# Experts in pairs, one in each column half of the array, over a ring of twelve staging slots

## What is computed

```python
N_EXPERTS, N_GROUPS, TOP_K, D_FF_EXPERT = 16, 4, 2, 512

def grouped_moe(h, router_w, router_bias, w_gate, w_up, w_down):
    t = h.reshape(B * S, D)                        # 256 tokens x 1024
    scores = sigmoid(t @ router_w)
    ...                                            # best group of 4 experts, the top 2 experts in it
    gates = ...                                    # 256 x 16, two entries a row are not zero
    for e in range(N_EXPERTS):
        he = silu(t @ w_gate[e]) * (t @ w_up[e])   # 1024 -> 512
        out = out + gates[:, e:e + 1] * (he @ w_down[e])   # 512 -> 1024
```

## Time and profile before

| | |
|---|---|
| runs | 2398.96, 2403.47, 2403.6 us; median 2403.47 |
| the profiled execution | 2399.3 us, of which the span is 2397.5 |
| TensorE busy / granted clock, mean | 2188.3 us (91%) / 0.955 |
| VectorE, ScalarE busy | 1468.1 us (61%), 884.0 us (37%) |
| DMA | 592.65 MB, mean 247 GB/s |
| first expert layer, first up matmul to the residual | 1660.54 to 1926.54 |
| second expert layer, the same | 2124.65 to 2388.08 |

### The profile page before, as it was taken

One profiled execution on the slowest core, in us unless ns is written; L12 is line 12 of the kernel. 1 busy time (PEld: TensorE's weight loads), 2 busy tenths in 40 slices (PEclk: granted clock), 3 DMA queues, 4 the chain that ended last, 5 costly groups with the idle time before them and its releaser, 6 DMA issues.

```text
span 2397.5 us, 28486 instructions
## 1 busy us (share of the span) xinstructions
PE 2188.3 (91%) x10492; PEld 1627.1 (68%) x10492; DVE 1468.1 (61%) x2294; ACT 884.0 (37%) x1093; POOL 62.3 (3%) x93
## 2 busy tenths in 40 slices
PE   3999899988998998999979998877999989889998
PEld 3788787867886887888867887654555467655553
DVE  6888777647896887766658986764212167532112
ACT  3344545544344343545534334421211244211111
POOL 0000000000000000000000001100000011000000
PEclk9999999999999999999999999877999989889999
DMA  8997443436995896444327993411999954149997
GB/s 345 387 375 306 157 165 141 139 112 236 367 370 196 322 376 245 175 150 152 130 88 292 362 363 130 154 42 55 373 388 396 407 195 159 45 149 379 390 386 292
DMA packets 86337, 592.65 MB, mean 247 GB/s; under 512 B 9680, under 2 KB 13136, under 8 KB 15568
## 3 DMA queue, kind: packets, MB, share of 16 engines
q1 hardware_dynamic: 79760, 579.90, 62.3%
q10 hardware_dynamic: 6464, 11.19, 1.4%
HBM read 590.00 MB, written 1.05 MB: 247 GB/s over the span
## 4 chain that ended last, share of the span: by engine, by line
PE 80%; DVE 10%; ACT 4%; DMA 3%; issue 2%; POOL 1%; DVEq 0%; SPq 0%; POOLq 0%; ACTq 0%
PE gu L2096 12%; PE acc L1807 11%; PE acc L1810 10%; PE acc L1811 10%; PE tr L2096 10%; PE gu L1807 6%; PE gu L1811 6%; PE gu L1810 6%; PE acc L2096 5%; PE tr L1870 3%; DVE w_lo L1000 2%; DMA proj<-ada_stream 2%; DVE proj L1072 1%; ACT pair L564 1%; DVE tf L1666 1%
## 5 line engine op out<-in xcount | busy, mean ns | idle before, releaser
L1000 DVE TENSOR_TENSOR w_lo<-stage,w_hi 128x2048 fp32r<-128x2048 f32 x240 | 547.9, 2286 | 57.9 <-ACT w_hi L526 57.6
L526 ACT ACTIVATE w_hi<-stage 128x2048 fp32r<-128x2048 f32 x240 | 457.3, 1911 | 273.3 <-PE acc L1811 261.1
L1072 DVE SCALAR_TENSOR_TENSOR proj<-proj,c_row 128x1024 f32<-128x1024 f32 x240 | 291.6, 1218 | 49.2 <-DMA proj<-ada_stream 39.2
L1807 PE MATMUL acc<-w_hi,hT_hi 128*128 128x512 f32 (+1 forms) x736 | 308.5, 419 | 6.2 <-DVE hT_lo L1368 5.1
L1807 PE MATMUL gu<-w_hi,hT_hi 128*128 128x512 f32 x704 | 283.0, 402 | 10.0 <-DVE pair L1148 9.5
L1810 PE MATMUL acc<-w_lo,hT_hi 128*128 128x512 f32 (+1 forms) x736 | 292.2, 397 | 0.0
L1811 PE MATMUL acc<-w_hi,hT_lo 128*128 128x512 f32 (+1 forms) x736 | 292.0, 397 | 0.0
L1811 PE MATMUL gu<-w_hi,hT_lo 128*128 128x512 f32 x704 | 277.6, 394 | 0.0
L1810 PE MATMUL gu<-w_lo,hT_hi 128*128 128x512 f32 x704 | 277.3, 394 | 0.0
L2096 PE MATMUL gu<-stage,got 128*64 128x512 f32 x1024 | 242.6, 606 | 1.6 <-DVE got L1220 1.6
L1807 PE MATMUL acc<-w_hi,yT_hi 128*128 128x512 f32 (+1 forms) x460 | 184.3, 401 | 14.0 <-DVE yT_lo L1580 5.7
(11 more groups left out here) (222 smaller groups left out, 2651.5 us busy)
## 6 DMA issues: line engine op xcount, KB each, us to landing
stage<-wstream SPq DMA_DIRECT2D x432, 1024.0 KB, 6.0
proj<-ada_stream SPq DMA_DIRECT2D x120, 1024.0 KB, 7.6
tf<-bgate_in ACTq DMA_DIRECT2D x12, 256.0 KB, 4.5
proj<-rel_in ACTq DMA_DIRECT2D x16, 192.0 KB, 2.4
proj<-t_in ACTq DMA_DIRECT2D x8, 192.0 KB, 3.6
z_mix<-c_in ACTq DMA_DIRECT2D x2, 512.0 KB, 8.1
x_tok<-x_in ACTq DMA_DIRECT2D x1, 1024.0 KB, 20.2
x_out<-x_tok SPq DMA_DIRECT2D x1, 1024.0 KB, 4.0
```

Source lines behind the costliest of these rows:

```text
L526: act.activation(w_hi[:, n % PARTS, :], stage[:, n % STAGES, :], ACT.Copy).then_inc(hi_ready, 1)
L1000: dve.tensor_tensor(w_lo[:, n % PARTS, :], stage[:, n % STAGES, :], w_hi[:, n % PARTS, :].bitcast(F32), ALU.subtract).then_inc(chunk_ready, 1)
L1072: ins = dve.scalar_tensor_tensor(w, w, 1.0, c_row[:], ALU.mult, ALU.mult, accum_out=dst)
L1807: ins = pe.matmul(dst, l_hi, r_hi, start=start, stop=False, skip_group_check=True)
```

## The change

- The sixteen experts become eight pairs (`PAIRS`). `up` and `down` put expert `2p` in one column half and expert `2p+1` in the other; each keeps all its row blocks, so nothing is left to add. A pair has twelve chunks, ordered in `wstream` two by two (the same part of both experts).
- SiLU and product now work on token rows straight out of `gu`, and `turn_hidden(p, j)` is two plain transposes of 128 x 128. `twin` is gone. `scatter` and `pickT` cover the 128 slots of a pair at once.
- Twelve staging slots: chunks 0 to 5 of a pair stay in `stage`, 6 to 11 go to `w_raw`, which lies over `w_hi` and `w_lo`. The first six chunks for `w_raw` wait for the last use of the split buffers (`pe_used`), every later one for the chunk twelve before it.
- `route` now makes the gate row; the counting matmuls write `acc` in place of `tr`; `select` is two operations in place of eight, and is issued a quad earlier.
- At the first layer's end the split of the next chunk stands ahead of the last pair's `y_high` and `y_low`.
- `moe_dense` is rewritten as well; which path is taken depends on the inputs, and these are the same.

```diff
 def moe_up_at / moe_down_at
+    return n0 + RING * p + 4 * j + 2 * half + e
+    return n0 + RING * p + 8 + 2 * h + e
...
+        w_raw = nc.alloc_sbuf_tensor_at("w_raw", [P, 2, PARTS, CW], F32, offset=w_at)
...
+            def expert_chunk(n, n0, i=0):
+                if not isinstance(i, int) or n - n0 >= RING:
+                    sp.wait_ge(chunk_ready, n + 1 - RING + RING * i)
+                elif n - n0 >= STAGES:
+                    sp.wait_ge(pe_used, n0 + PARTS)
+                else:
+                    sp.wait_ge(chunk_ready, n + 1 - STAGES)
...
 ScalarE, moe
+                for p in range(PAIRS):
+                    silu(p, 0)
+                    silu(p, 1)
+                    if p == PAIRS - 1 and end < n_chunks:
+                        act.wait_ge(chunk_ready, moe_up_at(n0, p, 1, 1, 1) + 1)
+                        hi(end)
+                    y_high(p, 0)
+                    y_high(p, 1)
...
 VectorE, moe
+                    if p == PAIRS - 1:
+                        dve.wait_ge(chunk_ready, moe_up_at(n0, p, 1, 1, 1) + 1)
+                        ahead(end)
+                    y_low(p, 0)
+                    y_low(p, 1)
...
 TensorE, moe
-                def sides(dst, src, first, last, n):
-                    for k in range(4):
-                        rows_ = slice(SLOTS * (k % 2), SLOTS * (k % 2) + SLOTS)
-                        ins = small_mm(dst[rows_, :], src(k), stage[:, n % STAGES, k * 512:(k + 1) * 512],
-                                       first and k < 2, last and k >= 2)
+                def up(p, j, half):
...
+                    for k in range(4):
+                        for e in range(2):
+                            rows_, at = slice(SLOTS * e, SLOTS * e + SLOTS), SLOTS * (2 * (p % 2) + e)
+                            ins = small_mm(gu[rows_, j, :], got[q % 2][:, 4 * half + k, at:at + SLOTS],
+                                           moe_tile(n + e, n0)[:, k * 512:(k + 1) * 512],
+                                           half == 0 and k == 0, half == 1 and k == 3)
...
-                    for c in range(8):
-                        at = (c // 4) * BLK + (c % 2) * P
-                        ins = small_mm(dst[:, c * SLOTS:(c + 1) * SLOTS], both[:, c // 2 % 2, at:at + P], cst("twin"))
+                    for c in range(2):
+                        ins = pe.transpose(dst[:, c * P:(c + 1) * P], both[:, j, BLK + c * P:BLK + (c + 1) * P], ident)
...
-                gate_row(b, b["u"])
...
+                for p in range(PAIRS):
+                    up(p, 0, 0)
+                    up(p, 0, 1)
+                    up(p, 1, 0)
+                    turn_hidden(p, 0)
+                    up(p, 1, 1)
+                    if p:
+                        scatter(p - 1, 0)
+                        scatter(p - 1, 1)
+                    extra(p)
+                    turn_hidden(p, 1)
+                    down(p, 0)
+                    down(p, 1)
+                scatter(PAIRS - 1, 0)
+                scatter(PAIRS - 1, 1)
...
 TensorE, route
+                    gate_row(b, b["u"] + 2)
+                    pe.wait_ge(sent_ready, step[1] + 1)
+                    bank, sent, before = acc[:, 0, :], rt[:, 3, :], cst("before")
```

More of the change, by code:

```diff
@@ L218, in moe_events, with moe_extra, moe_up_at, moe_down_at @@
         event("g", 0, r)
[L219 to L224, removed]
+    for p in range(PAIRS):
+        event("turn", p, 0)
+        for what in moe_extra(p):
             event(*what)
-    return tr_at
[L229 to L234, removed]
+        event("turn", p, 1)
+        event("y", p, 0)
+        event("y", p, 1)
+    return tr_at
+def moe_extra(p):
+    q, i = p // 2, p % 2
+    extra = [("pick", 0), ("weight", 0)] if p == 0 else []
     if q + 1 < QUADS:
-        extra.append(("g", q + 1, i))
+        extra += [("g", q + 1, 2 * i), ("g", q + 1, 2 * i + 1)]
         if i:
-            extra.append(("weight", q + 1) if i == 3 else ("pick", q + 1, i - 1))
+            extra += [("pick", q + 1), ("weight", q + 1)]
     return extra
 MOE_TR = moe_events()
[L243 to L253, removed]
+MOE_TURNS = len(MOE_TR)
+def moe_up_at(n0, p, j, half, e):
+    return n0 + RING * p + 4 * j + 2 * half + e
+def moe_down_at(n0, p, h, e):
+    return n0 + RING * p + 8 + 2 * h + e
+def staging_slots(plan):
+    used, slots = [0] * RING, []
+    first = [b["n"] for step, b in plan if step[0] == "ffn" and step[3]]
+    for n in range(plan[-1][1]["n"]):
+        c = [n - n0 for n0 in first if 0 <= n - n0 < 3 * MOE_BLOCKS]
+        slot = c[0] % RING if c and c[0] % RING >= STAGES else n % STAGES
+        slots.append((slot, used[slot]))
+        used[slot] += 1
+    return slots
 def hidden_turn(start, g):
@@ L271, in build @@
     n_chunks = plan[-1][1]["n"]
+    slots = staging_slots(plan)
+    moe_first = [b["n"] for step, b in plan if step[0] == "ffn" and step[3]]
     dense_steps = [(step[1], b["n"]) for step, b in plan if step[0] == "ffn" and not step[3]]
@@ L697, in moe_dense @@
[L697 to L701, removed]
+                for g in range(4):
+                    silu(g)
+                with act.Fori(0, PAIRS - 1) as i:
+                    for g in range(4):
+                        silu(4 + g, i)
+                act.nop().then_inc(th_ready, MOE_BLOCKS)
+                act.nop().then_inc(hi_ready, 3 * MOE_BLOCKS)
@@ L703, in heads @@
+                act.wait_ge(chunk_ready, end)
+                ahead(end)
             def heads(b, hd):
@@ new lines, in moe @@
+                select(0)
+                for r in range(4):
+                    take(("g", 0, r), flat(got[0][:, 2 * r:2 * r + 2, :]))
+                select(1)
+                for p in range(PAIRS):
+                    hidden(p, 0)
+                    turned(p, 0)
+                    hidden(p, 1)
+                    extra(p)
+                    turned(p, 1)
+                    if p == PAIRS - 1:
+                        dve.wait_ge(chunk_ready, moe_up_at(n0, p, 1, 1, 1) + 1)
+                        ahead(end)
+                    y_low(p, 0)
+                    y_low(p, 1)
```

489 lines of the change are left out of this document (226 added, 263 removed).

## The result

The changed kernel takes **2316.11 us**, the median of four runs from 2313.92 to 2320.71; before, in the same session, 2401.22 (2395.95 to 2403.6). The ratio is **0.9655, 95% interval 0.9638 to 0.9672**: 3.45% faster. Forecast were 2312, with a range from 2299 to 2352. The profiled execution took 2315.31 us, its span is 2313.5: 84.0 us less than the 2397.5 of before, where the sum forecast 89.4.

A forecast was written before the change was run, and what follows sets the result against it. TensorE was taken to pace the expert layers, with transfers binding after the change. Savings of 42.4, 41 and 6 us (89.4) took 2399.3 to 2309.9; 2 added for the median gave 2312 us, range 2299 to 2352.

The forecast's parts named there:

- The bound changes from TensorE to the transfers: Expert layers: a pair costs TensorE 24 to 27 us, its twelve chunks 29.8 us, so transfers become the pace.
- The transfers' pace: Expert layers: 2.485 us a chunk, from 422 GB/s in the last experts before the change.
- The rival of slow transfers: Expert layers: 2.71 us a chunk, layers of 240 and 244 us, kernel 2350 us; chance 15%.
- The last landing: Each expert layer: flow starts at 5.6 us, 84 chunks follow, the last lands 214.3 us after the first up.
- The ends: Last landing to residual: 9.7 us in the first layer; last down 3.4 and tail 2.4 in the second.
- coupling: Each expert layer: 1 us added for the unevenness of two paces that lie 3 us apart.
- Ahead of the layers: Before each expert layer: moved gate row and shorter `select` start the gather earlier, -3 us twice, bounds 0 and -4.
- TensorE's work: Each expert layer: matmuls, turns, scatters and extra rounds sum to 213.0 us, plus tail and first waits: 217 us.
- TensorE stays the bound: Expert layers: slots and even flow hide the transfers, layers of 217 and 221 us, kernel 2302 us; chance 8%.
- The rival of a falling clock: Expert layers: TensorE's waits lower the clock to a mean of 0.90, layers 241 and 245 us, kernel 2352; chance 9%.
- -42.4 and -41: Savings forecast for the second expert layer (263.4 to 221 us) and the first (266.0 to 225 us).
- -6: Ahead of both expert layers together: the forecast saving of 3 us taken twice.

The follow-up runs named there:

- less to load: Changed kernel, but chunks for the six slots of `stage` load only half their columns, TensorE's work whole (output not the reference's): 2279.83 us, ratio 0.9502.
- two slots more: Changed kernel with fourteen chunk slots, chunks 12 and 13 placed in `z_mix` and the place of `prob`: 2302.65 us, ratio 0.9599.
- no head start: Changed kernel, but chunks 6 to 11 of each expert layer wait for the release of the chunk six before: 2339.07 us, ratio 0.9755.
- the slots alone: Kernel before, experts one by one, with twelve slots and six chunks more loaded ahead of each expert layer: 2400.44 us, ratio 1.0014.
- the late split: Changed kernel with the next chunk's split back behind the last `y_high` and `y_low`: 2314.62 us, ratio 0.9648.
- six slots: Changed kernel's pairs over only the six slots of `stage`, with the split at its old, late place: 2363.61 us, ratio 0.9854.

## Why the prediction was right, and where it was off

**The bound changes from TensorE to the transfers**: right. Three runs carry it: less to load gives 35 us, two slots more give 12, no head start takes 23; and the slots alone, with TensorE's old work, give nothing.

**The transfers' pace**: right. 2.485 us a chunk was forecast from the 422 GB/s of one stretch; at the 421 to 422 GB/s of the windows after it is 2.49 us. The rival of slow transfers (15%, 2350) is out: the old 387 GB/s were demand, as the slots alone show. By the Trainium skill, "DMA: Bandwidth & Descriptors", section "Where 436 GB/s comes from", which says this without a condition on how many cores stream, the memory's side would have held the rate at about 358 GB/s; with one core at work no such limit shows over some 200 us a layer here.

**The last landing**: forecast 214.3 us after the first up; TensorE's last wait for one ends 218.1 us after it in the first layer (1875.18) and 217.0 in the second (2297.16). Here lie 2.7 to 3.8 us a layer, the main part of the miss. This is the term of the sum that was too small. The start was not: until 1664 the engines had moved 0.66 MB, which at 422 GB/s puts the start of the flow at 5.4 us after the first up, where 5.6 was forecast. The end was late. Up to 1875.06 the DMA engines had moved 219.06 us x 408 GB/s = 89.4 MB, while the 84 chunks are 88.1. So 1.3 MB, 1.2 chunks or 3 us of transfer, was mostly that of chunks further behind: with some nine in flight (23.4 us by 2.49 each) the last part of a chunk lands after the first parts of the next. In the second layer no chunk stands behind the last one, and there the same unevenness of the engines shows as a flow that tapers off:

```profile
2285.00:2293.00 8.00, 7.06 (x34) 3.22 (x30) 0.85 (x2) 0.39 (x1) 0.00 (x0) 1.00 1.02 421
...
2295.00:2297.16 2.16, 1.76 (x11) 0.34 (x7) 0.00 (x0) 0.29 (x1) 0.00 (x0) 1.00 0.33 137
```

Some engines have ended by then while others still work on the last chunk, which costs about 1.7 us against a full rate up to the end. Near the start of both layers the flow dips besides (392 GB/s from 1680 to 1690, 396 from 2100 to 2110), 0.6 to 0.7 us each. The working had only the transfers' sum and a landing time of chunks that had the engines to themselves.

**The ends**: second layer, 5.8 us from last landing to residual and 1 for coupling were forecast, 6.1 measured. First layer, 9.7 and 1 forecast, 10.5 measured. The order (`w_hi`, `w_lo`, `ylo`) was read rightly, and the late split shows its price, 1.8 us. That 10.5 comes so near 10.7 is partly luck: from the first `ylo` to the residual it was 3.9 us (1881.82 to 1885.72) where 3.0 were forecast, since the scatter came out of an idle stretch of 3.88 us and ran at a granted clock of 0.50 (from 1882.70 to 1886), and the 1 us for coupling paid for it.

**Ahead of the layers**: right. -3 was forecast twice. From the router's values to the first up it is 2.9 and 3.1 us less (20.3 to 17.4, 20.1 to 17.0); the whole parts outside the layers give 3.4 and 3.6, and 0.5 us is less than what these parts differ by between two profiles of the same kernel (first up at 1657.04 and 1659.50). The move of the gate row alone gives 2.1 and 1.4 of it; its loss to a lower clock in the gather, named as a possibility, is some 1.1 us and real.

**TensorE's work**: mis-sized by 8 us, in a step that didn't decide the time. 213.0 and 2.4 and 1 to 2 us were forecast, 209.4 measured. The rows of the run with less to load show where. The two turns of a pair were taken at 1.6 us; from the start of a turn to the next matmul it is 0.36 and 0.34, so 0.7 a pair, 7.2 us less in eight pairs. The weight round was taken at 1.8 us, by the 1.84 of the earlier trace rows; with 64 columns it takes 0.65, four times, 4.6 us less. Against this the six groups of a pair are 20.9 us (10.4, 3.6 and 6.9 from start to start) and not 20.6, some 2.5 us more in all, and the waits for copies by VectorE add up to 2.9 us in the layer, about 1.4 more than allowed. So the rival "TensorE stays the bound" had the wrong price: not 2302 but near 2280, by the run with less to load, and its place as the lower end of the range was too high.

**The clock**: 1.00 from 1656 to 1875, though TensorE waited 13 times, and 1.00 from 2080 to 2297. The rival of a falling clock (9%) is out here. The Trainium skill, "TensorE: Matmul & The Clock Gate", section on HAM oscillation, warns of waits for DMA between bursts; waits of at most 1.3 us did not bring it about. Longer waits go with it: with no head start a wait of 2.14 us ends at 1688.77, and from 1690 to 1692 the granted clock is 0.50 (0.91 from 1680 to 1700); with six slots waits of 2.13 and 2.06 us end inside the two windows at 0.94. The rival needed a starved queue.

In sum, -42.4 and -41 became -40.3 and -37.4, -6 became -7, and 0.8 us came back behind the second residual. The mechanism was right, and the miss of 4 us comes in the main from the last landing.

## What to carry to other kernels

When work is taken off the engine that sets the pace, work out the next bound before counting the saving: here the first layer lost 57 us of TensorE's time (266.0 to the 209.4 of the run with less to load) and gave 37. Once transfers bind, the useful knob is how much is loaded before the flow begins; each 1 MB chunk of idle memory found for it was worth 2.2 to 2.7 us a layer, and two such chunks made the fastest whole kernel of this study, 2302.65 us. The end of that road is TensorE's own 209.4 us a layer. For a flow with many chunks in flight, add about one chunk's transfer to the time of the last landing, as the 2.7 to 3.8 us here show.

## What I had not expected of the hardware

- A queue that is kept full delivers the sum on time but each chunk late: medians of 21.3 and 23.4 us to landing, where the transfer itself is 2.5, and some 3 us more than its turn for the last one of a layer.
- The sixteen records of a weight round took 1.84 us with a stationary matrix of 128 columns and 0.65 with 64, both at a granted clock of 1.00.
- The gather ran at 0.63 us a pair of records (granted clock 0.50) or at 0.40 (0.99), and reached the faster pace sooner where TensorE had worked just before it; taking work away ahead of it cost 1.1 us in it.
